# The S5 rotation table made among the mLSTM chunks of its own pass, in rows of the mixed tensor

## The reference

```
h = rmsnorm(x, norm_w[l]);  proj = h @ w_in[l]
s5_x, s5_g | hg_q, hg_f, hg_i, hg_g | ml_q, ml_k, ml_v, ml_o, ml_i, ml_f, ml_g | rt_q, rt_k, rt_v, rt_g = split(proj)
mixed = concat(s5 * silu(s5_g), hgrn * silu(hg_g), mlstm * silu(ml_g), retention * silu(rt_g))
x = x + mixed @ w_out[l]
```

## Time and profile before

| | us |
|---|---|
| median of 3 runs | 1565.33 |
| lowest, highest | 1562.23, 1573.06 |
| profiled execution, its own time | 1563.95 |
| its span | 1562.1 |
| TensorE busy | 1375.1 (88%) |
| VectorE busy | 887.8 (57%) |
| ScalarE busy | 551.8 (35%) |
| GpSimd busy | 450.3 (29%) |

### The profile page before, as it was taken

How to read it: one execution, slowest core, us unless ns; L and a number is a source line. 1 busy time by engine, 2 the same in 40 slices (tenths; PEclk the granted TensorE clock), 3 DMA queues, 4 the chain that set the end, 5 groups by cost and what they waited for, 6 DMA issues and landing times.

```text
span 1562.1 us, 31689 instructions
## 1 busy us (share of the span) xinstructions
PE 1375.1 (88%) x12391; PEld 1206.8 (77%) x12391; DVE 887.8 (57%) x2670; ACT 551.8 (35%) x1197; POOL 450.3 (29%) x628
## 2 busy tenths in 40 slices
PE   2868899989887898998999899998999899789886
PEld 2757788778776888886778789878878799779665
DVE  4986746464795516455655536646465444644546
ACT  4435443343323523322443234334433423321011
POOL 4342434431002433231310254443100533331001
PEclk9989899989998999998999999998999899999988
DMA  6222123431234332372313332343123314456501
GB/s 175 95 81 70 55 83 109 145 105 62 75 108 121 102 77 87 85 108 69 112 63 116 109 100 83 110 144 115 60 68 110 99 57 123 136 87 115 148 9 59
DMA packets 167563, 149.84 MB, mean 96 GB/s; under 512 B 63440, under 2 KB 155352, under 8 KB 165752
## 3 DMA queue, kind: packets, MB, share of 16 engines
q1 hardware_dynamic: 96696, 76.38, 18.3%
q10 hardware_dynamic: 70720, 71.44, 15.8%
HBM read 124.42 MB, written 23.37 MB: 95 GB/s over the span
## 4 chain that ended last, share of the span: by engine, by line
PE 61%; DVE 16%; ACT 6%; DMA 5%; issue 5%; POOL 4%; SPq 2%; DVEq 0%; ACTq 0%; POOLq 0%
PE psum L2347 17%; PE psum L2352 16%; PE psum L2681 5%; DVE r L1686 4%; PE psum L2659 3%; PE psum L2600 3%; DVE r L2060 3%; DMA wraw<-in_w_in 2%; POOL wlo L1152 2%; PE psum L2599 1%; ACT r L1467 1%; PE psum L2511 1%; PE psum L2419 1%; POOL rs L1177 1%; PE psum L2597 1%
## 5 line engine op out<-in xcount | busy, mean ns | idle before, releaser
L1152 POOL TENSOR_TENSOR wlo<-wraw,whi 128x256 fp32r<-128x256 f32 (+1 forms) x448 | 350.9, 819 | 414.2 <-ACT whi L1196 408.7
L2352 PE MATMUL psum<-whi,hhi 128*128 128x256 f32 (+1 forms) x896 | 272.2, 304 | 14.0 <-ACT th L1283 12.2
L2352 PE MATMUL psum<-whi,hlo 128*128 128x256 f32 (+1 forms) x896 | 262.9, 293 | 0.0
L2352 PE MATMUL psum<-wlo,hhi 128*128 128x256 f32 (+1 forms) x896 | 262.8, 293 | 0.0
L2347 PE MATMUL psum<-hhi,whi 128*128 128x288 f32 (+2 forms) x672 | 231.9, 345 | 7.0 <-ACT r L1317 4.8
L2347 PE MATMUL psum<-hhi,wlo 128*128 128x288 f32 (+2 forms) x672 | 220.5, 328 | 0.0
L2347 PE MATMUL psum<-hlo,whi 128*128 128x288 f32 (+2 forms) x672 | 220.3, 328 | 0.0
L2352 PEld LDWEIGHTS psum<-whi,hhi 128*128 128x128 f32 x896 | 181.1, 202 | 22.9 <-issue 14.9
L2352 PEld LDWEIGHTS psum<-wlo,hhi 128*128 128x128 f32 x896 | 181.1, 202 | 0.7 <-issue 0.5
L1174 POOL TENSOR_SCALAR rs<-mv 128x4 f32<-128x4 f32 (+1 forms) x54 | 10.4, 192 | 594.0 <-DVE mv L2243 591.3
L2352 PEld LDWEIGHTS psum<-whi,hlo 128*128 128x128 f32 x896 | 180.4, 201 | 0.0
(11 more groups left out here) (355 smaller groups left out, 2319.8 us busy)
## 6 DMA issues: line engine op xcount, KB each, us to landing
wraw<-in_w_in ACTq DMA_DIRECT2D x50, 1024.0 KB, 5.4
wraw<-in_w_out ACTq DMA_DIRECT2D x14, 1024.0 KB, 5.4
x<-xo SPq DMA_DIRECT2D x48, 128.0 KB, 2.3
r<-x SPq DMA_DIRECT2D x10, 512.0 KB, 5.3
r<-in_c_rot SPq DMA_DIRECT2D x4, 1088.0 KB, 7.5
wraw<-in_w_in ACTq DMA_DIRECT2D x4, 1056.0 KB, 6.2
r<-WTm SPq DMA_DIRECT2D x4, 1024.0 KB, 13.7
r<-VTm SPq DMA_DIRECT2D x4, 1024.0 KB, 6.3
```

The lines of the kernel that those rows point to most:

```text
L1152: nc.gpsimd.tensor_tensor(wlo[:, hslot[b], ks, 0:width], wraw[:, wslot[b], ks, 0:width], whi[:, hslot[b], ks, 0:width].bitcast(F32), ALU.s ...
L2352: mm = nc.tensor.matmul(bank.t[:, 0:width], x[:, kt, c], w[:, sl, kt, 0:width], start=first, stop=last)
```

## The change

E is no longer a part of `s5set`. The new function `rotations(n, stage)` puts its four parts, "e", "e2", "e3" and "e4" (the correction of the length, before a part of "e3"), into the mLSTM stage of pass n, n = 0 and 1, one behind the step "N" of each of chunks 0 to 3; so layer 1's table is now made in pass 1's mLSTM stage. E lies in rows 6 and 7 of mixT (row positions of retention) and its scratch in rows 0 and 1 (of S5). A step "se" behind the stage stores it. The other work of "e" (B and C loaded, C turned) is a step "c" in the old place. ScalarE waits for E before it writes the first S5 gate piece into mixT, and for the store of E before it writes retention's chunk 0 there; SyncE waits for the store before it loads Em.

```diff
     def s5set(l):
-        return [(("s5set", l), x) for x in ("e", "e2", "e3", "b", "va", "vb", "wa", "wb") + SET_PIECES + ("s",)] if "s5" in parts else []
+        return [(("s5set", l), x) for x in ("c", "b", "va", "vb", "wa", "wb") + SET_PIECES + ("s",)] if "s5" in parts else []
+
+    def rotations(l, steps):
+
+        for c, x in enumerate(("e", "e2", "e3", "e4")) if "s5" in parts and "ml" in parts else ():
+            k = steps.index((("ml", l, c), E_PLACE[l])) + 1
+            steps[k:k] = [(("s5set", l), x)]
+        return steps
...
-        plan += weave(mix(n, "ml"), beside)
+        stage = weave(mix(n, "ml"), beside)
+        plan += rotations(n, stage) + [(("s5set", n), "se")] * ("s5" in parts) if n < DEPTH else stage
...
+E_PLACE = ("N", "N")
...
-        cE = R2.take(2, 8, 64)
+        R2.take(2, 8, 64)
...
+        cE = mixT[:, 6:8, 0:HALF].rearrange("p r (q b) -> p r q b", q=8)
+        et = [mixT[:, i, 0:HALF] for i in range(2)]
...
+                if s[0] == "s5set" and part == "se":
+                    sp.wait_ge(*set_dve.at(s + ("E",)))
+                    sp.dma_start(Em[s[1]].rearrange("p (r b) -> p r b", r=2), mixT[:, 6:8, 0:HALF]).then_inc(*set_e.inc(s))
+                elif s[0] == "s5set" and part == "c":
...
-                    sp.wait_ge(*set_dve.at(s + ("E",)))
-                    sp.dma_start(Em[l], cE.rearrange("p r q b -> p (r q b)")).then_inc(*set_out.inc(s + (0,)))
...
+                        sp.wait_ge(*set_e.at(("s5set", l)))
...
+                    if k == (n, "s5_g", 0, 0) and n < DEPTH and s5sets:
+                        act.wait_ge(*set_dve.at(("s5set", n, "E")))
...
+                    if br == "rt" and c == 0 and n < DEPTH and s5sets:
+                        act.wait_ge(*set_e.at(("s5set", n)))
...
                         if part == "e":
+                            dve.wait_ge(*set_zero.at(set_zero.keys[-1]))
+                            if l:
+                                u = outs_of(l - 1)[-1]
+                                dve.wait_ge(*PB[bank_of[u]].full.at(u))
...
-                        for k in {"e": (1, 2, 4), "e2": (8, 16), "e3": (32,)}[part]:
-                            t, u = (x[:, 0:8 * k].rearrange("p (s k) -> p s k", k=k) for x in ct)
+                        for k in {"e": (1, 2, 4), "e2": (8, 16), "e3": (32,), "e4": ()}[part]:
+                            t, u = (x[:, 0:8 * k].rearrange("p (s k) -> p s k", k=k) for x in et)
```

More of the change, by code:

```diff
@@ L115, in groups @@
         for x in steps:
-            if out and (x[0][0] in ("final", "prenorm") or x[1] in ("A0", "AX", "A1", "P", "Q", "N", "u", "store", "e2", "e3", "b", "va", "vb", "wa", "wb") or x[1] is None or isinstance(x[1], tuple) and x[1][0] == "take"):
+            if out and (x[0][0] in ("final", "prenorm") or x[1] in ("A0", "AX", "A1", "P", "Q", "N", "u", "store", "e", "e2", "e3", "e4", "se", "b", "va", "vb", "wa", "wb") or x[1] is None or isinstance(x[1], tuple) and x[1][0] == "take"):
                 out[-1].append(x)
@@ L258, in make_plan @@
         opening.insert(opening.index((("proj", 0, "hg_i"), ("take", (0, "hg_i", 1)))) + 1, (("hgpre", 0), None))
-    plan = first + spread(opening, s5set(0)[:8]) + head[:1] + s5set(0)[8:12] + head[1:k] + s5set(0)[12:]
+    plan = first + spread(opening, s5set(0)[:6]) + head[:1] + s5set(0)[6:10] + head[1:k] + s5set(0)[10:]
     head = head[k:]
@@ L432, in trunk_kernel @@
             odd = s[0] not in ("final", "last") and s[1] % 2
-            if s[0] == "s5set" and part == "e":
+            if s[0] == "s5set" and part == "c":
                 aux_keys.append(s + ("C",))
@@ L1352, in _ @@
                     nc.scalar.activation(cs, ph, ACT.Sin, scale=-0.5, bias=C("halfpi")).then_inc(*vec_act.inc("sin"))
-                elif s[0] == "s5set" and part == "e":
+                elif s[0] == "s5set" and part == "c":
                     l = s[1]
@@ L1681, in _ @@
                     take_piece(part[1])
-                elif s[0] == "s5set" and part in ("p", "p2", "p3", "e", "e2", "e3", "b", "va", "vb", "wa", "wb"):
+                elif s[0] == "s5set" and part in ("p", "p2", "p3", "e", "e2", "e3", "e4", "b", "va", "vb", "wa", "wb"):
                     l = s[1]
```

14 lines of the change are left out of this document (7 added, 7 removed).

## The result

| | before | after |
|---|---|---|
| median, us | 1563.78 | 1589.76 |
| lowest, highest | 1561.32, 1573.06 | 1586.77, 1590.99 |
| runs | 4 | 4 |
| span of the profiled execution | 1562.1 | 1589.2 |
| granted clock of it | 0.935 | 0.926 |

The ratio is 1.0131 with a 95% interval of 1.0093 to 1.0169, which is 20 us, 15 to 26. The medians are 26.0 us apart and the two spans 27.1, so both lie at the upper end of the interval or just above it. I forecast 3 and a range that ended at 1582; the time is outside it.

A forecast was written before the change was run, and what follows sets the result against it. The prediction took TensorE to bound the kernel, with VectorE priced only where TensorE waits for it. Its terms, −11.5 − 6.5 + 8 + 9 + 4 = +3, gave a median of 1568.3 us, range 1552 to 1582.

The forecast's parts named there:

- What bounds the kernel: Whole kernel: TensorE holds 61% of the chain; VectorE instructions have a price only where TensorE waits for them.
- Term 1: Opening: with E gone the gates' op waits for ScalarE, not VectorE, and starts 9.9 us earlier; minus 11.5 in all.
- Term 2: Head of pass 1: VectorE has 12.9 us less before the flag, TensorE's waits of 1.00 and 4.00 go; minus 6.5.
- Term 3: mLSTM stage of pass 0: e and e2 delay score flags and a bank's release, e3 and e4 cost nothing; plus 8.
- Term 4: mLSTM stage of pass 1: cover is 0.16 and 0.27 us, e and e2 delay the score flags; plus 9.
- Term 5: Hand-over to retention: in pass 1 E's store lands late behind eight sample-state stores, and ScalarE waits; plus 4.
- The lock: VectorE and GpSimd share a port pair; a weight split beside each part of E gives 1583 us; chance 0.03.
- The serial rival: mLSTM stages and hand-over: both E blocks stand whole before TensorE, the store costs 13; +21, 1586 us; chance 0.12.
- The range: Whole kernel: half-widths 8, 6.5, 6, 5 and 6.5 added as squares to 14.5; 1552 to 1582 us, chance 0.75.

The follow-up runs named there:

- open_twice: The kernel before the change, with all products of layer 0's E computed twice in the opening; 1574.52 us (ratio 1.007).
- place_c: The changed kernel, with each part of E behind the chunk's scores (step C) in place of behind its y (step N); 1578.95 us (ratio 1.0059).
- no_e: The changed kernel, with 42 of the 45 instructions of E left out in each layer, stores and waits kept; 1557.49 us (ratio 0.9942).

## Why the prediction was wrong

*What bounds the kernel* was right in its method, and so was the sentence that cover in the mLSTM stages is 0.1 to 0.3 us. What came of it was priced too low, and one place of it was not looked at. By the traces the five terms came to −10.7, −1.1, +11.6, +17.5 and +7.1 where −11.5, −6.5, +8, +9 and +4 were forecast; with the +2.7 that belong to no term that is +27.1 for +3. Terms 2 and 4 are 14 of the 24 between.

*Term 1, minus 11.5.* Right: −10.7, and the op that was to start near 59 started at 58.78. The flag of W came at 89.46, the "near 90" of the text; the wait for it is gone, though I had expected it to keep its length. open_twice shows that this place has no slack the other way.

*Term 2, minus 6.5.* Wrong, and a step failed, not a size: "VectorE has 12.9 us less before the flag" was taken to mean that the waits for that flag go. The stretch is 1.1 shorter in the profile, and 1.1 in the means over all traces. The waits of 1.00 and 4.00 stand 7 and 42 us behind the flag of the block (427.20); I never asked who released VectorE in between. With E gone it waits for TensorE (the rows of 413.28 to 425.35 above, 7.1 us) and longer for the loads of x (1.62 and 2.62 us at 455.61 and 463.42, where before had 1.01), so most of the work taken away turned into idle time. Of the bounds 0 to −12.9 it came out next to the 0.

*Term 3, plus 8.* The places were right one by one: e 3.10, flag 1.05 late (1.2 forecast), a wait for the bank behind the take (4.6 forecast, 6.93 measured). The size failed in e2, priced 4 and measured 6.3, and in the clock, 0.7 forecast and 2.6 measured (11.6 less 9.0 of waits). Sum +11.6, inside the bound of 12.9.

*Term 4, plus 9.* The step that failed most: +17.5. "e3 and e4 follow chunks 2 and 3" was argued from pass 0, where it holds; in pass 1 a sample chunk follows chunk 3, e4 stands ahead of its scores, and nothing in the term prices that: it was put at nothing and measured 4.67 of wait. e2 was 5.28 of wait where 4 less cover was forecast, the two e waits (1.63 and 1.54) are the 3.3 forecast, and 4.4 is clock behind stalls of 5.3 and 4.7 us. The upper bound of 13 was no bound, since it held one block of 12.9 at undisturbed prices and no clock. In place_c, where no part stands behind a y, the stretch is 11.9 shorter.

*Term 5, plus 4.* The mechanism was right to its landing time (24.5 measured, 22.6 forecast), and in no_e the very matmul that was named, before's L2547 at 693.07, waits 5.76 where 5.5 was worked out. The size is 7.1. I took off for term 4's delay; but the delay moves the issue of the store as well, as the text itself says. In the changed kernel itself the stall without a semaphore stands in the same microseconds, and its length was in no term. Of the reason given, that SP's queue keeps its order, the trace has no more than the landing time: a load on ScalarE's queue, behind none of these stores, took as long (22.6).

*The lock.* From the first passage on the Trainium skill ("SBUF — State Buffer", "SBUF: two separate sides") and the factor of the earlier trace rows I had +17 for the sum if a split stood beside each part. It stood beside three of eight parts, the two e2 and pass 1's e4, and made them 3.2, 3.2 and 2.8 us longer. The rows of single products agree with the page: each one that meets the split ends just behind a split op. I had given this 0.03, as if all eight or none must meet it.

*The rivals.* The serial rival had 1586 and a chance of 0.12, and it comes nearest: 28 us of E's cost in the two stages (no_e) and 7.1 of hand-over, less the opening's 10.7. That is luck in part: of its terms the gains (−18, measured −11.8) and the store (13, measured 7.1) were 6 too large each. It was asked to decide by e3's and e4's gaps; it was decided by e2's slower price, the clock, and e4 in pass 1 alone.

*The range.* Five half-widths were added as squares, as if they were independent. They were not: terms 3 and 4 share what made each too low (the split beside VectorE, and the clock behind the stalls of 6.9 and 5.3 us), and the gain of term 2 was a hope of the same kind.

## What to carry to other kernels

Taking work from an engine gains only if that engine was not waiting for others between the work and the flag: list its own waits from there to the next wait of the bound engine before a saving is booked, and then check the new place in the same way, in every pass that has one more chunk. Prices of small VectorE ops must be taken from a row with the same neighbours on GpSimd, since a part that is moved meets what is there. For a moved DMA, look at how long its new neighbours on any queue take to land (22.6 us here, 5.2 for a load of the same size 33 us earlier), and where a part was free, a second of the same length may not be (13 us in the head).
